# A row scale computed first on GpSimd, stored and reloaded at once, and the bias table's transfers moved behind it

## The reference, cut to what matters

```python
h = rmsnorm(x, norm_mix[i])
z = h @ w_in[i]
q, k, v, b_g, c_g, xc = jnp.split(z, [...], axis=-1)
...
s = einsum(q, k) * scale + bias        # bias = rel_bias[t5_bucket(key_pos - query_pos)]
...
o_conv = b_g * short_conv3(c_g * xc, conv_w[i])
x = x + jnp.concatenate([o_att, o_conv], axis=-1) @ w_out[i]
```

## Time and profile before

| what | us |
|---|---|
| median of three runs | 607.11 |
| lowest and highest | 607.06 and 607.49 |
| the profiled execution | 605.1 |
| its span, first to last instruction | 603.3 |

### The profile page before, as it was taken

The page is one execution under the profiler, slowest core; times in us unless marked ns, Lnnn a source line. Parts: engine busy times, 40 slices in busy tenths (PEclk is TensorE's granted clock), DMA queues, the critical chain, the costliest instruction groups (busy, mean ns, idle before and its releaser), DMA issues.

```text
span 603.3 us, 8730 instructions
## 1 busy us (share of the span) xinstructions
PE 595.0 (99%) x3160; PEld 490.7 (81%) x3160; DVE 419.5 (70%) x781; ACT 329.3 (55%) x595; POOL 68.8 (11%) x109
## 2 busy tenths in 40 slices
PE   9999999999999999999999999999999999999997
PEld 6888989888887787888877887778888888878886
DVE  5522993354552566746878789899999999688863
ACT  6851030222232676656556566789999998961211
POOL 0250000000000000100100113242221220210000
PEclk9999999999999999999999999999999999999999
DMA  8945827120212412213324677999999999775611
GB/s 330 373 71 189 315 105 273 36 74 31 77 63 71 183 36 105 71 70 106 106 72 143 249 255 257 389 371 415 411 410 410 413 411 374 290 297 205 221 47 65
DMA packets 39042, 126.52 MB, mean 210 GB/s; under 512 B 6448, under 2 KB 7472, under 8 KB 38968
## 3 DMA queue, kind: packets, MB, share of 16 engines
q1 hardware_dynamic: 33224, 112.97, 51.1%
q0 software_dynamic: 4896, 12.59, 5.4%
q10 hardware_dynamic: 880, 0.41, 0.2%
HBM read 113.33 MB, written 23.10 MB: 226 GB/s over the span
## 4 chain that ended last, share of the span: by engine, by line
PE 80%; DMA 8%; DVE 6%; POOL 2%; issue 1%; ACT 1%; SPq 1%; ACTq 0%; DVEq 0%; POOLq 0%
PE bank L508 19%; PE bank L510 18%; PE bank L509 18%; PE bank L1929 7%; PE bank L1946 3%; PE bank L1965 3%; PE bank L538 3%; PE bank L540 3%; PE bank L539 3%; DMA x_T<-in_xT 2%; DMA row_scale<-x_rstd 2%; POOL bias_sb L801 2%; PE bank L2240 1%; PE bank L2080 1%; DMA pick<-moe_rows 1%
## 5 line engine op out<-in xcount | busy, mean ns | idle before, releaser
L503 DVE TENSOR_TENSOR w_split<-w_raw,w_split 128x1024 fp32r<-128x1024 f32 x33 | 40.5, 1229 | 21.8 <-ACT w_split L498 21.6
L508 PE MATMUL bank<-w_split,moe_xT 128*128 128x512 f32 x120 | 48.5, 404 | 0.8 <-DVE w_split L1700 0.8
L510 PE MATMUL bank<-w_split,moe_xT 128*128 128x512 f32 x120 | 47.0, 392 | 0.0
L509 PE MATMUL bank<-w_split,moe_xT 128*128 128x512 f32 x120 | 46.8, 390 | 0.0
L1018 ACT ACTIVATE sq_tmp<-bank 128x512 f32<-128x512 f32 x12 | 7.2, 598 | 69.7 <-PE bank L510 69.7
L498 ACT ACTIVATE w_split<-w_raw 128x1024 fp32r<-128x1024 f32 x33 | 34.5, 1051 | 19.1 <-DMA w_raw<-in_w_in 18.8
L985 ACT ACTIVATE s<-s,mn 128x512 f32<-128x512 f32 (+1 forms) x48 | 30.9, 645 | 18.7 <-DVE mn L1436 18.7
L508 PE MATMUL bank<-w_split,x3T 128*128 128x512 f32 (+1 forms) x104 | 39.4, 379 | 0.5 <-DVE x3T L1878 0.5
L487 DVE TENSOR_TENSOR w_split<-w_raw_more,w_split 128x1024 fp32r<-128x1024 f32 x32 | 38.0, 1217 | 2.7 <-ACT w_split L481 2.7
L510 PE MATMUL bank<-w_split,x3T 128*128 128x512 f32 (+1 forms) x104 | 38.9, 374 | 0.0
L509 PE MATMUL bank<-w_split,x3T 128*128 128x512 f32 (+1 forms) x104 | 38.8, 373 | 0.0
(11 more groups left out here) (321 smaller groups left out, 1594.6 us busy)
## 6 DMA issues: line engine op xcount, KB each, us to landing
w_raw<-in_w_moe SPq DMA_DIRECT2D x32, 512.0 KB, 15.0
w_raw_room<-in_w_moe SPq DMA_DIRECT2D x30, 512.0 KB, 16.0
w_raw_more<-in_w_moe SPq DMA_DIRECT2D x30, 512.0 KB, 16.4
w_raw<-in_w_in SPq DMA_DIRECT2D x23, 512.0 KB, 9.4
pick<-moe_rows SPq DMA_DIRECT2D x12, 512.0 KB, 5.0
bias_rows<-bias_table SPq DMA_DIRECT2D x1, 4096.0 KB
w_raw<-in_w_out SPq DMA_DIRECT2D x8, 512.0 KB, 3.4
toep<-bias_rows SPq DMA_DIRECT2D x4, 896.0 KB, 7.0
```

What stands on the lines that cost most here:

```text
L503: nc.vector.tensor_tensor(W[:, u % WS, 1], raw(u)[0], f(W[:, u % WS, 0]), ALU.subtract).then_inc(lo_done, 1)
L508: nc.tensor.matmul(out, hi, whi, start=first, stop=False)
L509: nc.tensor.matmul(out, lo, whi, start=False, stop=False)
L510: return nc.tensor.matmul(out, hi, wlo, start=False, stop=last)
```

## The change

GpSimd takes the row scale ahead of the bias table: the three instructions that were behind the 31 are now in front, behind the wait for the squares, and the wait for the constants comes after them. SP issues the store of the row scale at u = 8 as before, but without the wait for the bias table ahead of it, waits for its landing right there (on a semaphore of its own, row_scale_stored) and reloads it at once, where the reload stood at u = 10. The store of the bias table moves from u = 8 to u = 13, the copy to bias_rows from u = 10 to u = 15. ScalarE's wait for the row scale moves from ahead of CONV_B's evictions to the first product of Q_B, the first place where ScalarE reads what GpSimd made. The counts of the waits for b_st are lowered to match.

```diff
@@ sync
                 if u == 8:
-                    sp.wait_ge(g_sum, 1 + len(RUNS))
-                    sp.dma_start(bias_dram, bias_sb[:]).then_inc(b_st, 16)
                     sp.wait_ge(g_xr, 2)
                     with nc.allow_non_contiguous_dma(reason="one value of a token"):
-                        sp.dma_start(scale_dram.rearrange("i p -> p i"), x_rstd[:]).then_inc(b_st, 16)
-                if u == 10:
-                    sp.wait_ge(b_st, 32)
+                        sp.dma_start(scale_dram.rearrange("i p -> p i"), x_rstd[:]).then_inc(sc_st, 16)
+                    sp.wait_ge(sc_st, 16)
                     for q in range(2):
                         sp.dma_start(rs[q][:], bass.AP(scale_dram.tensor, q * SEQS[0], [[0, P], [1, SEQS[q]]])
                                      ).then_inc(rs_ld, 16)
+                if u == 13:
+                    sp.wait_ge(g_sum, 2 + len(RUNS))
+                    sp.dma_start(bias_dram, bias_sb[:]).then_inc(b_st, 16)
+                if u == 15:
+                    sp.wait_ge(b_st, 16)
                     sp.dma_start(bias_rows, bass.AP(bias_dram.tensor, 0, [[REL, MAPS], [0, P], [1, REL]])
                                  ).then_inc(b_st, 16)
                 if u == 20:
...
-                    sp.wait_ge(b_st, 48)
+                    sp.wait_ge(b_st, 32)
                     sp.wait_ge(a_xq, TILES)
                     toeplitz(0)
@@ gpsimd
             pool.memset(mhalf[:], -0.5).then_inc(g_sum, 1)
             pool.wait_ge(g_sum, 1)
+            steps = [1]
+            def inv_root(ss, n, e):
+                ...
+            pool.wait_ge(a_xq, TILES)
+            pool.tensor_scalar(x_veps[:], x_rstd[:], EPS, EPS, ALU.add, ALU.mult).then_inc(g_xr, 1)
+            inv_root(x_rstd[:], TILES, EPS).then_inc(g_xr, 1)
             pool.wait_ge(c_ld, 16 * 6)
             for k, c0, c1 in RUNS:
                 pool.tensor_scalar(bias_sb[:, c0:c1], relb[:, k:k + 1].broadcast_to([MAPS, c1 - c0]),
                                    -1.0, None, ALU.mult).then_inc(g_sum, 1)
-            steps = [1 + len(RUNS)]
...
-            pool.wait_ge(a_xq, TILES)
-            pool.tensor_scalar(x_veps[:], x_rstd[:], EPS, EPS, ALU.add, ALU.mult).then_inc(g_xr, 1)
-            inv_root(x_rstd[:], TILES, EPS).then_inc(g_xr, 1)
+            steps[0] += len(RUNS)
@@ scalar
             split_hi(6)
             split_hi(7)
-            act.wait_ge(g_xr, 2)
...
                     elif b in (Q_B, K_B):
                         r = n - TILES * Q_B
+                        if r == 0:
+                            act.wait_ge(g_xr, 2)
                         act.wait_ge(pe_acc, n + 1)
@@ vector
                 if i == 0:
-                    dve.wait_ge(b_st, 48)
+                    dve.wait_ge(b_st, 16)
```

9 lines of the change are left out of this document (5 added, 4 removed).

## The result

The changed kernel takes **603.64 us** in the median of 14 executions (602.64 to 605.15). The kernel before, on the same chip, takes 606.48 (605.08 to 610.30, 14 executions). The ratio is 0.9948, with a 95% interval of 0.9931 to 0.9965. The forecast was 606.1, with a range from 605.2: the change is faster, and by more than the range allowed. Two executions of the kernel before, of all that were timed in this study, took 1527 us and are left out throughout.

What follows compares the result with a forecast made beforehand. TensorE's matmul stream was taken as the bound, with two stops on one row-scale thread; 0.70 + 0.27 us gained, the copy's move 0, so 607.11 - 0.97 = 606.1 us, range 605.2 to 607.4.

Steps and rivals of the forecast that it cites:

- both stops: TensorE's stops of 0.70 us at product n = 6 (40.38 us) and 0.27 us at n = 9 (57.09), forecast to go.
- one thread on GpSimd and SP: Chain of waits from 25.7 to 57.1 us: bias table, root, store, reload, squares, multiplies, then TensorE's product n = 9.
- The first rival: Slower: row scale's store, with SP held behind it, outlasts 11.04 us and the reload lands late; 610.8 us, chance 0.05.
- The fourth: Root delayed beside VectorE's splits and a slow reload leave the second stop; only 0.70 won, 606.4 us, chance 0.08.
- The third: No change: the gain is given back at a later place that keeps its own time; 607.1 or 606.8 us, chance 0.17.
- the last line of the sum: Whole kernel: the 2.0 us between profiled execution and median carried over unchanged, so 607.11 - 0.97 = 606.1 us.
- the stops' sum: TensorE near 40 and 57 us: two stops of 0.70 and 0.27 us, read off one profile, give 0.97 us.
- The second rival: Faster: timed executions have a longer stop near 57 us, perhaps from a varying store, all removed; 605.1 us, chance 0.20.
- -0.70 from ScalarE's wait: Moving ScalarE's wait behind the c_T evictions frees product n = 6's bank early, starting it at 39.68: 0.70 us won.
- -0.27 from the rest: Earlier root, store and reload free product n = 9's bank at 52.0 us, with 4.1 us slack: 0.27 us won.
- Part 5: Moving the 4 MB copy bias_rows from ahead of unit 11 to behind unit 15 on SP's queue, said to cost 0.
- a 0.3 us loss avoided: At unit 11's first use (78.30 us), slack 0.7 under the 0.97 won: the copy left in place would eat about 0.3 us.

Runs made afterwards that it cites:

- the delayed kernel: The changed kernel with four roots that nobody reads put on GpSimd ahead of the true one: 604.84 us, ratio 0.9962.
- Part 1 alone: The kernel before with only ScalarE's wait for the row scale moved to the first query product: 605.05 us, ratio 1.0003.
- GpSimd's order alone: The kernel before with only the row scale put ahead of the bias table on GpSimd, SP's order kept: 610.08 us, ratio 1.0056.
- the early copy: The changed kernel with the bias table's store at u = 8 and its copy at u = 10: 603.67 us, ratio 0.9962.
- Late constants: Six constant loads issued behind the split of unit 5: in the kernel before 612.05 us, ratio 1.0084; in the changed kernel 603.68 us, ratio 0.9955.
- with the wait and without any copy in the way: The kernel before with the bias table's store and copy late and ten fills replacing the table, still waiting for the constants: 606.12 us, ratio 1.0004.
- a late copy alone: The changed kernel with four unread roots ahead of the true one, bias table's store at u = 8 and copy at u = 10: 608.72 us, ratio 1.0036.
- without the wait: The kernel before with bias store and copy late, the table not waiting for the constants and reading another tile: 605.51 us, ratio 0.9979.

## Why the prediction was wrong

**What held.** The place and the mechanism: both stops gone, both from one thread on GpSimd and SP. The times forecast for the changed kernel came in: root at 33.1 (measured 32.5), reload at 49.4 (48.3), product n = 6 at 39.7 (39.8), no wide step at 56.1, copy at 61.4 (60.8), ScalarE never waiting for unit 16. The first rival fell, since the squares began 15.8 us behind the store's issue and not 20.4 or more. The fourth fell, since the root was not held up: it ran from 31.19 to 32.54, from 31.61 on beside a split, and took the same 1.35 us as before. The third fell too: what was won at 57 us is there at 234.9, and the median keeps it.

**The step that failed** is the last line of the sum: the profiled execution gives -0.97, and the 2.0 us between it and the median are carried over whole, as if they lay outside the thread. The working had the two halves of an answer (the thread has no slack; timed executions are longer than the profiled one) and didn't join them. A thread that sets TensorE's end makes every delay ahead of it into time, and the change takes all of them at once. Against the profiled execution the sum is nearly right: 605.10 - 0.97 = 604.1, where the changed kernel's median is 603.64. The forecast of 606.1 missed it by 2.5 us, which can be divided into three. First, 607.11 was the median of three executions that all lay above 607, where 42 of 143 do; against 605.9, the median of the 143, it was 1.2 us too high, by the luck of the draw. Second, the remaining 0.8 us between 605.1 and 605.9 were carried over, and none of it stayed. Third, the changed kernel lies 0.5 us under the profiled execution less 0.97. So the size of the miss is in part luck; the gain isn't, since it was 2.2 us by that median, 2.8 beside the 14 and 0.97 in the sum.

**The term mis-sized** is the stops' sum. 0.97 us was read off one execution; over six it is 0.66 to 1.68, 1.15 in the mean, with a third stop near 78 us in three of them. Up to the attention output the six profiles lie 1.5 us behind the changed kernel; the 0.4 us beyond the stops wasn't located. The profiled execution was among the shortest of the 14 timed beside it (605.10 against 605.08 to 610.30). The prediction knew that it lay 2.0 us under the median shown, and this was the sign to ask which of its waits could be longer.

**The second rival** had the sign, the reason ("the change removes all of it") and a part of the cause. It named a store that varies. Store and reload do vary in the kernel before, by 0.5 us over six profiles, and in one of them they hold the difference in the second stop. No run shows them behind the executions above 609.7, and the delayed kernel, which has them on its path, stays within 1.1 us. The rival allowed a microsecond more; it is 1.2 to 1.9 us more in the median.

**The parts** were added as if each had a share: -0.70 from ScalarE's wait, -0.27 from the rest. That is wrong as a split. Part 1 alone gives nothing clear of noise and can be left out; GpSimd's order alone costs 3.4 us by its ratio; the early copy or the late one gives the same. The two stops lie in a row on one thread, so the first can't be won without the second. The prediction said so itself ("hangs on the same thread") and still priced them apart.

**Part 5** was called free with a 0.3 us loss avoided. The loss avoided isn't where the prediction put it: with the copy issued at 46.7 as a result of the early reload there is no loss to avoid, and before the change the place already cost up to 0.82 us in three of six profiles.

**What stays open.** No profile fell on an execution above 607 us. In the traces here the clock fell only with stops of 3.44 us and more, so TensorE probably stopped for long somewhere in those above 609.7; that it did so for the constants' landing, the table's length, the transfers of the row scale or the copy is shown only by edits. Late constants cost 5.1 us in the kernel before by the ratio (6.2 by the medians) and none in the changed one. There is no long execution among 60 of the changed kernel and its variants with an early root (602.64 to 605.22); by the share of 18 in 143 that would be chance in 3 cases of 10,000. There are two near 610 with the wait and without any copy in the way, and a spread of 4.7 us from a late copy alone. None in 12 without the wait says little, as said above. How much each gives isn't settled, and what delays a landing wasn't seen. Nor is it settled why the delayed kernel keeps so much of the gain.

## What to carry to other kernels

When the profiled execution lies under the median of the timed ones, look in it for a chain without slack that hangs on a landing or on a contended engine: the change that takes such a chain off the path wins the spread too, of which the profile shows one draw. A median of three is a draw as well: here it stood 1.2 us above that of 143. Stops that lie one behind the other on one thread are one term, which goes as a whole or not at all; and a value that many wait for must be made early and stored early in one edit, because an early root behind a late store on the same queue was slower than no change. Several profiles of the kernel before cost little and would have shown 0.66 to 1.68 us where one showed 0.97.

## What the hardware showed that was not expected

**The clock after a stop.** TensorE's granted clock fell to half, its lower level of 1.2 GHz, with stops of 3.44 and 6.12 us, and stayed at 1.00 in and behind stops of 2.42 us and less. In the longer one it was down while TensorE still stood: the stretch from 42.6 to 43.6 us, without a matmul, has 0.50. With late constants the matmuls behind the stop start 0.43 us apart instead of 0.23, and the row of 44 to 48 us has 0.50. The attention output then starts at 242.44, 7.7 us behind the 234.7 of the kernels without a stop, of which the stop is 6.12: the clock took most of the other 1.6 us. With GpSimd's order alone it is 240.09, 5.4 us behind for a stop of 3.44.

**A load's landing is not its issue.** Six small loads issued 6.8 us earlier landed 1.3 us earlier, while the DMA engines were full (share 1.03 from 9 to 24 us).

**GpSimd beside VectorE.** The same 31 instructions took 8.1 to 9.2 us where the root or late constants had pushed them past most of VectorE's splits and 10.3 to 12.0 beside them, where instructions of 14 columns lasted 1178 ns in the mean instead of 256 in the changed kernel. The Trainium skill, "SBUF — State Buffer", section "Who interferes with whom", has the rule (a VectorE instruction with two SBUF inputs against a GpSimd one that reads SBUF); the trace agrees for the bias table. The root in the changed kernel, which reads SBUF too, ran beside a split for 0.9 us, and neither lasted longer than alone (1.35 and 1.22 us).
